# Routing tables of a mixture-of-experts layer: the two fixed experts' row numbers and gathers are taken ahead of the general tables

## The reference

```python
h2 = rmsnorm(x, norm_ffn[l]).reshape(b * s, D_MODEL)
g_p, g_idx = lax.top_k(softmax(h @ w_rg + b_rg), 1)          # one of 4 groups
e_top, e_loc = lax.top_k(e_in, 2)                            # two of its 8 experts
order = jnp.argsort(flat_e)                                  # tokens sorted by expert
xs = h[slot_tok].reshape(n_blocks, MOE_BLOCK, d)             # blocks of 128 tokens of one expert
ys = (silu(xb @ w_gate[e]) * (xb @ w_up[e])) @ w_down[e]     # per block, width 256
x = x + segment_sum(ys * slot_w, slot_tok)
```

## Time and profile before

| | us |
|---|---|
| median of 3 runs | 2567.05 |
| lowest and highest | 2566.03 and 2567.2 |
| the profiled execution | 2570.07 |
| its span, first to last instruction | 2568.3 |
| busy in it: PE, VectorE, ScalarE, POOL | 2326.3, 1205.7, 896.0, 176.4 |
| mean granted TensorE clock (1 is full speed) | 0.958 |

### The profile page before, as it was taken

How to read it: one execution, slowest core, us unless ns; L and a number is a source line. 1 busy time by engine, 2 the same in 40 slices (tenths; PEclk the granted TensorE clock), 3 DMA queues, 4 the chain that set the end, 5 groups by cost and what they waited for, 6 DMA issues and landing times.

```text
span 2568.3 us, 31688 instructions
## 1 busy us (share of the span) xinstructions
PE 2326.3 (91%) x11166; PEld 1422.0 (55%) x11166; DVE 1205.7 (47%) x2666; ACT 896.0 (35%) x1842; POOL 176.4 (7%) x355
## 2 busy tenths in 40 slices
PE   5999989798999999999589998997989999899993
PEld 3476434565665556666345653445657655566662
DVE  4435388876663341111334344788666623311115
ACT  2122278854452101111122313797645511111113
POOL 0000032000000000000200000420000000000002
PEclk9999999899899989999789999998999999899996
DMA  6010001220100059999711000014010010799995
GB/s 254 25 56 27 33 14 42 85 58 1 50 1 26 26 202 358 421 423 422 306 44 46 33 27 33 17 51 128 2 50 1 1 36 33 293 396 422 422 422 220
DMA packets 101110, 353.86 MB, mean 138 GB/s; under 512 B 20246, under 2 KB 39660, under 8 KB 76396
## 3 DMA queue, kind: packets, MB, share of 16 engines
q1 hardware_dynamic: 89456, 310.15, 31.1%
q0 software_dynamic: 11520, 41.95, 4.3%
HBM read 296.03 MB, written 55.91 MB: 137 GB/s over the span
## 4 chain that ended last, share of the span: by engine, by line
PE 67%; DVE 12%; issue 7%; DMA 6%; ACT 5%; POOL 1%; PEldq 1%; PEld 1%; SPq 1%; DVEq 0%; ACTq 0%; POOLq 0%
PE bank L811 11%; PE bank L1269 10%; PE bank L1161 9%; PE bank L814 7%; PE bank L891 7%; PE bank L800 5%; DMA w_ring<-in_expert_w_gate 5%; PE bank L1290 5%; PE bank L923 4%; ACT group_arena L1550 2%; DVE group_arena L2016 2%; DVE residual L2396 1%; PE bank L1178 1%; PE bank L1223 1%; DVE group_arena L1791 1%
## 5 line engine op out<-in xcount | busy, mean ns | idle before, releaser
L811 PE MATMUL bank<-w_ring,normed_cols 128*128 128x260 f32 (+4 forms) x1280 | 437.3, 494 | 12.0 <-ACT heads_cols L1575 10.0
L811 PEld LDWEIGHTS bank<-w_ring,normed_cols 128*128 128x128 f32 x1280 | 238.6, 192 | 182.1 <-issue 154.6
L814 PE MATMUL bank<-normed_cols,w_ring 128*128 128x512 f32 x640 | 284.2, 604 | 7.4 <-ACT group_arena L1452 6.4
L800 PE MATMUL bank<-ident,group_arena 128*128 128x128 f32 (+1 forms) x1200 | 183.5, 296 | 117.3 <-DVE group_arena L1791 94.3
L800 PEld LDWEIGHTS bank<-ident,group_arena 128*128 128x128 f32 (+1 forms) x1200 | 147.4, 151 | 161.6 <-issue 83.5
L1269 PE MATMUL bank<-w_ring,group_arena 128*128 128x256 f32 x1024 | 228.6, 381 | 5.2 <-ACT group_arena L1689 3.5
L1161 PE MATMUL bank<-w_ring,heads_cols 128*128 128x512 f32 x512 | 225.5, 595 | 2.0 <-DVEq L263 2.0
L1269 PEld LDWEIGHTS bank<-w_ring,group_arena 128*128 128x128 f32 x1024 | 192.6, 190 | 50.7 <-issue 16.9
L814 PEld LDWEIGHTS bank<-normed_cols,w_ring 128*128 128x128 f32 x640 | 122.9, 194 | 161.2 <-issue 153.0
L891 PE MATMUL bank<-group_arena 96*128 96x512 f32 (+7 forms) x384 | 163.5, 532 | 24.7 <-ACTq L1440 12.6
L1290 PE MATMUL bank<-heads_cols,group_arena 128*64 128x512 f32 (+1 forms) x512 | 173.8, 596 | 2.8 <-DVE group_arena L2355 2.8
(11 more groups left out here) (351 smaller groups left out, 3081.8 us busy)
## 6 DMA issues: line engine op xcount, KB each, us to landing
heads_cols<-in_expert_w_down SPq DMA_DIRECT2D x64, 1024.0 KB, 15.4
w_ring<-in_expert_w_gate SPq DMA_DIRECT2D x32, 1024.0 KB, 17.5
w_ring<-in_expert_w_up SPq DMA_DIRECT2D x32, 1024.0 KB, 19.6
normed_cols<-in_expert_w_gate SPq DMA_DIRECT2D x32, 1024.0 KB, 14.7
normed_cols<-in_expert_w_up SPq DMA_DIRECT2D x32, 1024.0 KB, 18.6
expert_rows<-group_arena SPq DMA_DIRECT2D x48, 512.0 KB, 15.8
w_ring<-in_w_in SPq DMA_DIRECT2D x6, 2048.0 KB, 9.1
expert_rows<-heads_cols SPq DMA_DIRECT2D x1, 8192.0 KB, 27.7
```

Source lines behind the costliest of these rows:

```text
L800: last = pe.transpose(bank(4 + r % 2)[0:rows, col:col + src.shape[0]], src, ident[0:src.shape[0], 0:src.shape[0]])
L811: m = pe.matmul(out[:, 0:width], HT[:, k, part * P:(part + 1) * P], w, start=(k == 0), stop=(k == K - 1))
L814: m = pe.matmul(out[0:width, :], w, HT[:, k, part * HALF:(part + 1) * HALF], start=(k == 0), stop=(k == K - 1))
```

## The change

- PE counts a second time with the two columns of `M12` of experts 0 and 1 only (`early_ranks`, into bank 2), in two parts, each ahead of the general counts. VectorE makes from it a key (the rank of each token in its expert, or a far number for a token that did not choose it), compares the key with the row numbers (`early_hot`), and PE multiplies the result by the token numbers (`early_place`, 8 matmuls with one column each). VectorE copies the two columns into `early_i`, and POOL's first two gathers use these.
- The general tables follow as before on VectorE, but behind the early ones. Their 16 matmuls (`all_places`) move into the first unit, between its gate half and its up half, and write bank 6 instead of bank 2. The third gather waits for them (`idx_ready`).
- VectorE is busy with the tables when the rows of unit 0 are turned, so ScalarE takes both halves of them. `places_read` keeps PE from overwriting banks 0 and 1 before VectorE has read them.
- The fillers change from 14, 9, 24, 28 to 14, 4, 7, 16; `row_of_slot`, `blk_of_slot` and `blk_hot` move in the scratch area, away from what unit 0 writes.

```diff
-        WAIT_CHOICE, WAIT_ORDER, WAIT_TABLES, WAIT_ROWS = 14, 9, 24, 28
+        WAIT_CHOICE, WAIT_EARLY, WAIT_ORDER, WAIT_ROWS = 14, 4, 7, 16
...
-                pool.wait_ge(idx_ready, 1)
                 for u in range(UNITS):
...
+                    if u < QUAD_SINGLES:
+                        pool.wait_ge(early_idx, u + 1)
+                    elif u == QUAD_SINGLES:
+                        pool.wait_ge(idx_ready, 1)
                     if u >= QUAD_UNITS:
                         pool.wait_ge(x_turned, u - QUAD_UNITS + 1)
+                    rows = early_i[:, u:u + 1] if u < QUAD_SINGLES else idx_i[:, at:at + 1]
...
+                def early_ranks(a, b):
+
+                    n, w = b - a, QUAD_SINGLES
+                    if a == 0:
+                        pe.matmul(early, ones_h[0:EXPERTS, :], far_h[0:EXPERTS, :], start=True, stop=False)
+                    m = pe.matmul(early[:, a * w:b * w].rearrange("p (t e) -> p t e", t=n), before[:, :], M12[:, a:b, 0:w],
+                                  start=False, stop=False)
+                    for t in range(a, min(b, T - 1)):
+                        m = pe.matmul(early[:, (t + 1) * w:].rearrange("p (t e) -> p t e", t=T - 1 - t), ones_h[:, :],
+                                      M12[:, t:t + 1, 0:w].to_broadcast([P, T - 1 - t, w]), start=False, stop=t == T - 2)
+                    return m
+
+                def early_place(e):
+
+                    pe.wait_ge(early_hot_set, e + 1)
+                    for t in range(T):
+                        m = pe.matmul(early_bank(e)[:, 0:1], early_hot[:, e, :, t], tok_h[:, t:t + 1],
+                                      start=(t == 0), stop=(t == T - 1))
+                    m.then_inc(early_placed, 1)
...
                 pe.wait_ge(v2p, 4)
+                early_ranks(0, ROUTED[-1][0])
                 ranks(0, ROUTED[-1][0])
                 keep_busy(WAIT_CHOICE)
                 pe.wait_ge(v2p, 5)
+                early_ranks(ROUTED[-1][0], T).then_inc(early_counted, 1)
                 ranks(ROUTED[-1][0], T).then_inc(p2v, 1)
+                keep_busy(WAIT_EARLY)
+                for e in range(QUAD_SINGLES):
+                    early_place(e)
                 keep_busy(WAIT_ORDER)
                 pe.wait_ge(v2p, 6)
                 places().then_inc(p2v, 1)
 
-                keep_busy(WAIT_TABLES)
-                for k in range(2):
-                    pe.wait_ge(v2p, 7 + k)
-                    for t in range(T):
-                        m = pe.matmul(bank(2)[:, 0:SLOT_ROWS], row_hot[:, k, :, t], blk_hot[:, k, :, t],
-                                      start=(k == 0 and t == 0), stop=(k == 1 and t == T - 1))
-                m.then_inc(p2v, 1)
+                def all_places():
+
+                    for k in range(2):
+                        pe.wait_ge(v2p, 7 + k)
+                        for t in range(T):
+                            m = pe.matmul(bank(6)[:, 0:SLOT_ROWS], row_hot[:, k, :, t], blk_hot[:, k, :, t],
+                                          start=(k == 0 and t == 0), stop=(k == 1 and t == T - 1))
+                    m.then_inc(p2v, 1)
...
                         m.then_inc(done, 1)
+                        if isinstance(u, int) and u == 0 and half == 0:
+                            all_places()
...
                 keep_busy(WAIT_ROWS)
+                pe.wait_ge(places_read, 1)
                 turn_x_lo(0, 0, 1)
...
                 take_x(0, 0)
+                act.wait_ge(x_turned, 1)
+                act.activation(xgT[:, 0, 4:8, :], bank(1).rearrange("p (k n) -> p k n", k=4), ACT.Copy).then_inc(x_hi, 1)
...
+                chain(dve.memset(far_h, EARLY_FAR / EXPERTS))
...
+                dve.wait_ge(early_counted, 1)
+                chain(dve.scalar_tensor_tensor(early_key.rearrange("p e t -> p t e"), M12[:, :, 0:QUAD_SINGLES], -EARLY_FAR,
+                                               bank(2)[:, 0:QUAD_SINGLES * T].rearrange("p (t e) -> p t e", t=T),
+                                               ALU.mult, ALU.add))
+                for e in range(QUAD_SINGLES):
+                    chain(dve.tensor_tensor(early_hot[:, e, :, :], row_of_slot,
+                                            early_key[:, e:e + 1, :].to_broadcast([P, P, T]), ALU.is_equal))
+                    dve.sem_inc(early_hot_set, 1)
+
+                def early_rows(e):
+                    dve.wait_ge(early_placed, e + 1)
+                    dve.tensor_copy(early_i[:, e:e + 1], early_bank(e)[:, 0:1]).then_inc(early_idx, 1)
+
+                early_rows(0)
                 dve.wait_ge(p2v, 5)
...
                 dve.sem_inc(v2p, 1)
+                early_rows(1)
...
                 chain(dve.tensor_tensor(rank[:, :, :], cande[:, :, :], placed, ALU.add))
+                dve.sem_inc(places_read, 1)
...
-                chain(dve.tensor_copy(idx_i, bank(2)[:, 0:SLOT_ROWS]))
+                chain(dve.tensor_copy(idx_i, bank(6)[:, 0:SLOT_ROWS]))
...
-
-                take_x(0, 0)
```

More of the change, by code:

```diff
@@ L230, in trunk @@
         idx_ready = sem("idx_ready")
+        early_counted = sem("early_counted")
+        early_hot_set = sem("early_hot_set")
+        early_placed = sem("early_placed")
+        early_idx = sem("early_idx")
+        places_read = sem("places_read")
         over_idx = sem("over_idx")
@@ L481, in trunk @@
         row_hot = g(12288, T * P, dt=F16).rearrange("p (k n t) -> p k n t", k=2, n=P)
-        row_of_slot = g(13312, T * P // 2, dt=F16).rearrange("p (n t) -> p n t", n=P)
-        blk_of_slot = g(13824, T * SLOT_ROWS // 2, dt=F16).rearrange("p (n t) -> p n t", n=SLOT_ROWS)
-        blk_hot = g(14336, T * SLOT_ROWS, dt=F16).rearrange("p (k n t) -> p k n t", k=2, n=SLOT_ROWS)
+        row_of_slot = g(13568, T * P // 2, dt=F16).rearrange("p (n t) -> p n t", n=P)
+        blk_of_slot = g(14336, T * SLOT_ROWS // 2, dt=F16).rearrange("p (n t) -> p n t", n=SLOT_ROWS)
+        blk_hot = g(14496, T * SLOT_ROWS, dt=F16).rearrange("p (k n t) -> p k n t", k=2, n=SLOT_ROWS)
         slot_at = g(15104, 2 * T, dt=F16).rearrange("p (a b) -> p a b", a=2)
@@ L505, in trunk, with early_bank @@
         idx_cur = g(16740, 1, dt=I32)
+        early_i = g(16744, QUAD_SINGLES, dt=I32)
+        early_key = g(16748, T * QUAD_SINGLES // 2, dt=F16).rearrange("p (e t) -> p e t", e=QUAD_SINGLES)
+        early_hot = g(2592, T * P, dt=F16).rearrange("p (e n t) -> p e n t", e=QUAD_SINGLES, n=P)
+        far_h = g(3616, T, dt=BF16)
+        EARLY_FAR = 1000.0
+        def early_bank(e):
+            return bank((6, 2)[e])
         xg = g(4096, QUAD_UNITS, D)
@@ L753, in _ @@
                     at = unit_block(u // QUAD_UNITS, s)
+                    if u < QUAD_SINGLES:
+                        pool.wait_ge(early_idx, u + 1)
+                    elif u == QUAD_SINGLES:
+                        pool.wait_ge(idx_ready, 1)
                     if u >= QUAD_UNITS:
                         pool.wait_ge(x_turned, u - QUAD_UNITS + 1)
+                    rows = early_i[:, u:u + 1] if u < QUAD_SINGLES else idx_i[:, at:at + 1]
                     pool.indirect_dma_start(
                         out=xg[:, s, :], out_offset=None, in_=h2_dram,
-                        in_offset=bass.IndirectOffsetOnAxis(ap=idx_i[:, at:at + 1], axis=0)).then_inc(xg_in[s], 16)
+                        in_offset=bass.IndirectOffsetOnAxis(ap=rows, axis=0)).then_inc(xg_in[s], 16)
                 pool.wait_ge(idx_ready, 2)
@@ L1191, in _ @@
                 route_tile(T - 1)
+                early = bank(2)[:, 0:QUAD_SINGLES * T]
+                def early_ranks(a, b):
[14 more added lines that the diff above has]
+                    m.then_inc(early_placed, 1)
                 def ranks(a, b):
```

## The result

| | before | after |
|---|---|---|
| median, us (8 runs each) | 2567.64 | 2553.23 |
| lowest and highest of the runs | 2566.03 and 2572.75 | 2549.47 and 2560.45 |
| the profiled execution, us | 2570.07 | 2556.27 |

What follows compares the result with a forecast made beforehand. PE at 35.1 us a quad, with DMA close by at 37.3, was taken as the bound; gains of 6.05 us in layer 1 and 6.35 in layer 2 made 12.4, giving a median of 2554.7 us, range 2550 to 2563.

Steps and rivals of the forecast that it cites:

- Items 1 to 3: Ahead of unit 0: early counts on PE, keys and one-hots, queued VectorE work; gather 0 issued 9.2 us earlier.
- Item 4: Landing of gather 0: 6.2 us after issue, so PE turns rows 9.0 us earlier in layer 1, 9.3 in layer 2.
- Items 5 and 6: ScalarE copying the second half of the rows costs 0.05 us; the table product inside unit 0 costs 1.4 us.
- Item 7: PE's pauses before unit 0 bring half clock onto it: 1.5 us a layer, between 0 and 1.7.
- Item 8: Third gather, now waiting for the tables, is late for nobody, with 1 to 3 us in hand.
- Item 9: Later quads: the gain carries, as weight loads move earlier with PE; the 2.2 us a quad lost at the end stay.
- Quick rows: Gather 0 is there when the fillers end, clock holds: 8.6 us a layer, 17.2 in all, 2549.9; chance 7%.
- Late rows, cold PE: Gather 0 lands in 8.4 us, unit 0 at half clock: 2.9 us a layer, 6 in all, 2561; chance 17%.
- The DMA side keeps the gain: Refills do not move, PE waits longer in the last quads by what it won: 2567, no change; chance 9%.
- The 0.3 us that it would add: At gather 0: GpSimd cannot write descriptors while VectorE holds their shared port; adds 0.3 us.
- Slower: Gather 0 gets behind the queued weights; a landing of 15 us loses 3.7 us a layer, 2574.5; chance 6%.

Runs made afterwards that it cites:

- the second set: The changed kernel with the 16 table products done twice inside unit 0; the stages' sum is 3.2 us more.

## Why the prediction was right, point by point

**The forecast** of 12.4 us stood against 13.9 by the ratio (9.0 when run again), 13.8 between the two profiled executions and 12.0 in the two stages, of which 10.0 are the work of the mechanism that it describes. That mechanism was right; two terms were off in size, the early counts and the landing. That the whole came out so near is in part luck.

- *Items 1 to 3.* The gather is issued 8.4 and 9.3 us earlier against the last choice, where 9.2 was forecast. The missing 0.8 in layer 1 is the early counts (in layer 2 they are as late, but there the gather of before was later, too), 0.85 us later than forecast because the fillers ahead of them ran at 0.34 us each. I had put 0.5 us of small counts on the path and taken the fillers to be in time. The fillers ahead of the rows ended at 950.33, 15.5 after the last choice, where 14.5 was forecast.
- *Item 4, the landing, mis-sized:* 6.2 us forecast, 7.3 and 7.2 measured. The step that failed is its ground, the gather at 993.6: "it too was issued into a half-emptied queue". The DMA share was 0.98 in 992 to 994 us and 1.03 in the next two; the weights ahead of that gather landed 2.5 and 5.1 us after its issue, and those ahead of gather 0 in the changed kernel 3.5 and 6.7 us after. So more was queued ahead. The run with fewer fillers showed a landing tied to those weights, and the one with 1 MB less ahead showed 4.6 us. So PE turned 7.2 and 8.4 us earlier, not 9.0 and 9.3. The Trainium skill (DMA: Bandwidth & Descriptors, Queues, rings and completion order) says that each DMA engine takes turns between the queues that have work for it. The traces agree in part: once its first packets moved, the gather shared the engines with the weights, and in the loaded stage one overtook weights issued 8 us before it. But for 3 us after its issue no packet of gather 0 moved while the weights did, where 1.9 us passed with 1 MB less ahead; why is open. The 3.2 us for such a gather (the section Anatomy of one DMA — SWDGE (gpsimd) path) were reached by none in these runs: the shortest landing was 4.1 us.
- *Items 5 and 6.* Unit 0 starts 1.90 us after the turn (1.95 before): ScalarE's second copy costs nothing. Between the halves are 1.10 us; the second set alone costs 1.26 and 1.4 was forecast.
- *Item 7, the clock:* 1.5 forecast. The gate half took 5.24 and 5.30 us against 3.69 with the clock held, 1.6 us; the unedited kernel run again had 6.62 in one layer. From the start of unit 0 to that of unit 1, items 6 and 7 together, are 2.86 and 2.90 us more than before, as forecast (2.9).
- *Item 8.* 2.65 us in hand, within 1 to 3.
- *Item 9, borne out.* The gain did carry, and there are three long waits for weights as before. Unit 1 starts 4.35 and 5.56 us earlier, 9.9 in all, and the last store is issued 10.0 earlier: from unit 1 to it are 280.58 / 280.06 before and 280.26 / 280.31 after, so the pattern moved as a whole. The fourth expert's weights are issued 20.5 us after the last choice (955.33) and 26.2 before, 5.7 earlier, 1.4 more than PE's lead in layer 1, and this brought nothing that shows. A delay of them has its price, 2.3 us a layer for some 4. One reading was wrong without effect: the first load that PE paces is not that of 985.15 but the gate weights issued at 971.87, when unit 0 is done.
- *Sum.* Up to the last store the change brought 10.0 us instead of 12.4, short by the landing and the late counts. The 2.1 us of the last store's landing and the 1.8 outside the stages lie on top of it; no run shows them to be effects of the change. The prediction came close because what it missed and what it did not foresee nearly cancel.

**The rivals.** *Quick rows* did not happen in the changed kernel, but its mechanism exists: with 1 MB moved back the fillers decide, the clock holds, and the ratio is 0.9925. *Late rows, cold PE* lay nearer than its 17%: 7.3 lies between the forecast and its 8.4, and the run with the gather held back shows it (9.2 us of landing, gate half 5.82). *The DMA side keeps the gain* is excluded for the changed kernel by that same run and by the one with more fillers, where 1.56 and 1.85 us won by unit 1 reach the end whole; but with the second expert's down weights moved back 2.3 of the 7.7 us won by unit 1 are kept. The 0.3 us that it would add for VectorE's operations beside the gather are not shown: gather 0 took 1.22 us, as the first gather did before, but the second, at 946.74 and with VectorE's small operations beside it as well, took the usual 0.94. *Slower* at a landing of 11.3 us did not come near.

## What to carry to other kernels

Look at what was issued in the 20 us before a small transfer on the critical path, and move what is not needed first behind it; here 1 MB of weights moved back was worth 5.4 us, where the whole change had gained 12.0 in the same stages. It need not pay where much more is ahead: in the later quads a gather took 7.9 to 9.8 us and landed before weights issued ahead of it. Where an engine wait is shortened, check what fills the rest of it: a pause of 2.1 us ahead of the first real matmuls cost 1.6 us at half clock, and eight more fillers took that away. When two sides are closely matched, follow the lead of each separately: the weights 4 us later cost 2.3 us a layer, and 2 us sooner gained nothing that shows. And before a gain is put down to the change, follow it from stage to stage: here 2.1 of 12.0 us turned out to be the landing of one store 280 us later.

## What the runs showed of the hardware that was not expected

- The landing of a 0.5 MB gather depended on the weights ahead of it: 7.3 us, 8.9 when issued 1.5 us sooner, 4.6 with 1 MB less ahead. In the first case its queue moved no packet for 3 us. Yet with far more queued ahead, at 1151.36, a gather took 8.4 us and landed before weights issued 8 us sooner.
- The last store of 0.5 MB landed in 3.64 to 3.78 us where an instruction packet moved within it, and in 2.62 to 2.64 where none did. The cause is not shown.
- Idle times of 2.09 and 0.78 us of PE, with 1.1 us of turns between them, were followed by a granted clock of 0.51 and 0.64 in the next 4 us. With 0.59 and 0.78 the gate half took 3.69 us, and the length of the half clock varied between runs of one kernel (5.24 and 6.62 us for the same sixteen matmuls).
